# Zero products ahead of the second weight panel: one sequence of three for eight FFNs and three mixers, in place of a table per FFN

## The reference

```python
def swiglu(h, w_gate_up, w_down):
    gate, up = jnp.split(h @ w_gate_up, 2, axis=-1)
    return (jax.nn.silu(gate) * up) @ w_down
```

## Time and profile before

| | |
|---|---|
| median of 3 runs | 2603.05 us (2591.95 to 2603.62) |
| profiled execution, its own time | 2603.65 us |
| its span, first to last instruction | 2601.8 us |
| TensorE busy | 2495.0 us, 96% of the span, 23182 matmuls |
| VectorE busy | 1778.3 us, 68% |
| ScalarE busy | 1259.3 us, 48% |
| mean granted TensorE clock | 0.982 |

### The profile page before, as it was taken

How to read it: one execution, slowest core, us unless ns; L and a number is a source line. 1 busy time by engine, 2 the same in 40 slices (tenths; PEclk the granted TensorE clock), 3 DMA queues, 4 the chain that set the end, 5 groups by cost and what they waited for, 6 DMA issues and landing times.

```text
span 2601.8 us, 54597 instructions
## 1 busy us (share of the span) xinstructions
PE 2495.0 (96%) x23182; PEld 2436.6 (94%) x23182; DVE 1778.3 (68%) x2300; ACT 1259.3 (48%) x1508; POOL 216.0 (8%) x246
## 2 busy tenths in 40 slices
PE   7999759999999899999999999999999999999998
PEld 7999759999999889989999999999999998999998
DVE  5988966556555666657666669876657667986665
ACT  5434445334566653344344346565335335665433
POOL 5000050003000100000000000500000000320000
PEclk9999879999999999999999999999999999999999
DMA  5553014555677735535545544434555554443553
GB/s 214 183 189 125 19 67 176 180 191 169 187 174 182 174 117 193 192 133 189 192 172 206 193 171 154 147 130 165 191 183 185 191 193 147 152 147 146 179 194 127
DMA packets 65839, 430.76 MB, mean 166 GB/s; under 512 B 8288, under 2 KB 11360, under 8 KB 15904
## 3 DMA queue, kind: packets, MB, share of 16 engines
q1 hardware_dynamic: 58864, 410.30, 44.1%
q0 software_dynamic: 6000, 17.46, 4.5%
q10 hardware_dynamic: 832, 0.92, 0.1%
HBM read 426.45 MB, written 1.15 MB: 164 GB/s over the span
## 4 chain that ended last, share of the span: by engine, by line
PE 88%; DVE 7%; ACT 3%; issue 1%; DMA 0%; DVEq 0%; ACTq 0%
PE psum L2020 26%; PE psum L2022 26%; PE psum L2021 26%; DVE w_lo L1332 1%; ACT w_hi L847 1%; PE psum L2070 1%; PE psum L2235 1%; PE psum L2141 1%; PE psum L2384 1%; DVE h L1351 1%; PE psum L2372 1%; DVE h_lo L1340 1%; PE psum L2362 1%; PE psum L2124 0%; PE psum L2328 0%
## 5 line engine op out<-in xcount | busy, mean ns | idle before, releaser
L2020 PE MATMUL psum<-h_hi,w_hi 128*128 128x256 f32 x4320 | 1215.1, 281 | 16.4 <-DVE h_lo L1376 9.6
L2021 PE MATMUL psum<-h_lo,w_hi 128*128 128x256 f32 x4320 | 1205.0, 279 | 0.0
L2022 PE MATMUL psum<-h_hi,w_lo 128*128 128x256 f32 x4320 | 1204.6, 279 | 0.0
L847 ACT ACTIVATE w_hi<-raw 128x2048 fp32r<-128x2048 f32 x387 | 741.2, 1916 | 857.1 <-PE psum L2022 857.1
L1332 DVE TENSOR_TENSOR w_lo<-raw,w_hi 128x2048 fp32r<-128x2048 f32 x387 | 886.8, 2292 | 386.9 <-ACT w_hi L847 386.5
L2020 PEld LDWEIGHTS psum<-h_hi,w_hi 128*128 128x128 f32 x4320 | 816.1, 189 | 26.0 <-issue 20.8
L2021 PEld LDWEIGHTS psum<-h_lo,w_hi 128*128 128x128 f32 x4320 | 815.8, 189 | 0.6 <-issue 0.5
L2022 PEld LDWEIGHTS psum<-h_hi,w_lo 128*128 128x128 f32 x4320 | 815.5, 189 | 0.0
L2020 PE MATMUL psum<-act_hi,w_hi 128*128 128x256 f32 x1536 | 427.3, 278 | 0.7 <-DVE act_lo L1895 0.7
L2021 PE MATMUL psum<-act_lo,w_hi 128*128 128x256 f32 x1536 | 426.1, 277 | 0.0
L2022 PE MATMUL psum<-act_hi,w_lo 128*128 128x256 f32 x1536 | 426.0, 277 | 0.0
(11 more groups left out here) (342 smaller groups left out, 2386.5 us busy)
## 6 DMA issues: line engine op xcount, KB each, us to landing
raw<-in_panels SPq DMA_DIRECT2D x387, 1024.0 KB, 4.8
arena<-bias_by_distance POOLq DMA_DIRECT2D x32, 384.0 KB, 6.2
x<-in_x SPq DMA_DIRECT2D x1, 1024.0 KB, 5.6
arena<-in_s_cbd POOLq DMA_DIRECT2D x4, 256.0 KB, 3.0
arena<-in_s_b SPq DMA_DIRECT2D x1, 1024.0 KB, 15.2
arena<-in_s_c SPq DMA_DIRECT2D x1, 1024.0 KB, 17.2
hidden<-in_s_cbd POOLq DMA_DIRECT2D x4, 256.0 KB, 2.8
arena<-arena POOLq DMA_DIRECT2D x32, 32.0 KB, 1.9
```

Source lines behind the costliest of these rows:

```text
L847: a.activation(w_hi[:, s, :], raw[:, s, :], ACT.Copy).then_inc(hi_ready, 1)
L2020: t.matmul(o, w[0], xin[0], start=start, stop=False, skip_group_check=True)
L2021: t.matmul(o, w[0], xin[1], start=False, stop=False, skip_group_check=True)
L2022: return t.matmul(o, w[1], xin[0], start=False, stop=stop, skip_group_check=True)
```

## The change

The table goes. One sequence, `PACE`, is used in all eight FFNs and in the second panel of both Fourier mixers and of the GLU: the reduced-precision product of 64 columns of zeros ("wide") at (0, 0) and at (0, 4), and the plain fp32 product of two columns ("narrow") at (1, 4). All of them add zeros, so that no result changes.

```diff
-        FFN_LEADS = [{(1, 0): 1}, {(1, 0): 2}, {(0, 4): 0}, {(0, 2): 0, (1, 2): 0}, {(0, 0): 3, (1, 0): 0},
-                     {(0, 0): 2}, {(0, 0): 3, (1, 0): 1}, {(0, 0): 3, (0, 4): 3, (1, 4): 0}]
+        PACE = {(0, 0): True, (0, 4): True, (1, 4): False}
...
-            def lead(o, start=True, form=0):
-                z = zeros[:, :].bitcast(F32)
-                if form == 0:
+            def lead(o, start, wide):
+                if wide:
+                    t.matmul(o[:, 0:E], zeros[:, :], zeros[:, 0:E], start=start, stop=True, skip_group_check=True)
+                else:
+                    z = zeros[:, :].bitcast(F32)
                     t.matmul(o[:, 0:2], z, z[:, 0:2], start=start, stop=True, skip_group_check=True)
-                elif form == 1:
-                    t.matmul(o[:, 0:1], z, z[:, 0:1], start=start, stop=True, skip_group_check=True)
-                elif form == 2:
-                    t.matmul(o[:, 0:S].rearrange("p (a m) -> p a m", a=2), z[0:E, :],
-                             z[0:E, :].unsqueeze(1).to_broadcast([E, 2, P]), start=start, stop=True, skip_group_check=True)
-                else:
-                    t.matmul(o[:, 0:E], zeros[:, :], zeros[:, 0:E], start=start, stop=True, skip_group_check=True)
...
-                project(n0 + 1, 1, led=FFN_LEADS[f])
+                project(n0 + 1, 1, led=PACE)
...
-                    project(st["n0"] + p, p, parts=None if p else (dft_lo_ready, f * KT // 2), frees=(p == 3), led={(0, 0): 0} if p == 1 else None)
+                    project(st["n0"] + p, p, parts=None if p else (dft_lo_ready, f * KT // 2), frees=(p == 3), led=PACE if p == 1 else None)
...
-                    project(st["n0"] + p, p, parts=None if p else (s5_g_lo_ready, 0), frees=(p == 7), led={(0, 0): 0} if p == 1 else None)
+                    project(st["n0"] + p, p, parts=None if p else (s5_g_lo_ready, 0), frees=(p == 7), led=PACE if p == 1 else None)
```

## The result

| | before | changed |
|---|---|---|
| median of 7 runs each | 2603.05 us (2591.95 to 2605.40) | 2578.68 us (2577.45 to 2582.98) |
| profiled execution, own time / span | 2603.65 / 2601.8 us | 2578.26 / 2576.4 us |
| ratio to before, 95% interval | | 0.991 (0.9887 to 0.9933) |

The kernel is 24.4 us faster. The forecast was 2585, the range began at 2580: the direction and the mechanism of the three FFNs were right, the size was not, and the time lies 1.3 us under the range.

The account below looks back on a forecast made before the run. TensorE, busy 96% of the span, was taken as the bound through the spacing of its products. The sum 2603.65 - 20.0 + 0.72 + 0.75 = 2585.1 us was given as 2585, range 2580 to 2599.

Parts of the forecast that it names:

- FFNs 0, 1 and 5 turn quick: From (1, 4) of panel 1, 1500 products per FFN go from 117.8 to 113.3 ns: 6.67 us each, 20.0 saved.
- Turn quick later: FFNs 2, 3, 4, 6 and the three mixers reach the quick pace later, losing 162 products: 0.72 us added.
- the products of zeros themselves: In eight FFNs and three mixers, the zero products cost 4.92 us instead of 4.17: net 0.75 us added.
- I cost this at nothing: In FFN 0, VectorE's low part still arrives before the panel needing it, 0.6 us to spare: no cost.
- Rival 3: FFN 0 falls back to slow after TensorE waits for VectorE at the fifth panel: 2591 us, chance 0.05.
- Rival 1: The narrow product misses in one or two places, each slow FFN costing 6.67 us: 2592 to 2598, chance 0.22.
- rival 2: Something else sets the pace in FFNs 0, 1 and 5, so only costs remain: 2604.4 us, chance 0.08.
- Rival 4: At (1, 4) the narrow product misses where the old table hit, FFNs and mixers turning slow: up to 2634, chance 0.07.
- For this part, which no row prices, I take 4 us to either side.: Stretches between the FFNs at 1.2 GHz can fall differently once everything moves by 7 to 20 us: 4 us either way.

Follow-up runs that it names:

- the early variant: Changed kernel with its sequence replaced by one wide product at (0, 1) and the narrow one at (0, 2), all eleven places: 2630.1 us, 1.0111 of before.

## Why the prediction was right in kind and wrong in size

*"FFNs 0, 1 and 5 turn quick", 6.67 us each:* right. 6.61 measured in each of the three, and in each FFN that changed its pace in any later trace.

*"Turn quick later", 0.72, and "the products of zeros themselves", +0.75:* right, 1.4 measured for the two.

*"I cost this at nothing", VectorE in FFN 0:* right, with 0.5 us to spare where 0.6 were worked out: the low part was there at 90.54 + 2.29 = 92.83, its panel started at 93.32. Rival 3 did not happen. The two lines of the changed kernel:

```profile
90.54 2.29 DVE L1332 TENSOR_TENSOR w_lo<-raw,w_hi 128x2048 fp32r<-128x2048 f32 x1
...
93.32 0.28 PE L2018 MATMUL psum<-h_hi,w_hi 128*128 128x256 f32 x1
```

*Rival 1, a miss in one or two places:* not in the five traces with this sequence, that is in none of 55 places. That was luck in part: the reason given, three hits of three, was a weak one, and the sequence works by the table above, which three rows could not show. The gap in it is a stream that is already quick ahead of the wide product at (0, 4). That happened once, in FFN 0 of the trace with two narrow products, whose sequence is the same up to (1, 4), and there the first narrow one missed: one of 66 places in all.

*Rivals 2 and 4:* rival 2 is out by the first windows view and by the runs with one or two FFNs changed. Rival 4's mechanism exists: the early variant and the narrow product alone are slower than before because the narrow product comes at the wrong place. The changed sequence is not such a case.

*The step that failed* is the base under the sum: "For this part, which no row prices, I take 4 us to either side." It took all stages without a changed product as they were in the one profiled execution, and their shift in time as noise around zero. One of them was no noise. The S5 mixer's start ran at 1.2 GHz for 6.8 us in the kernel before, in both traces, behind a pause of TensorE of 1.48 us. In the three traces of the changed kernel FFN 0 ended some 6 us earlier, the pause was there, and the clock stayed up: 4.3 us in one direction between the profiled pair, 3.1 of them the fall itself. With that term the sum is 2581, inside the range. Why the clock stays up when FFN 0 ends then is open; the runs show only which end times went with which outcome. The other 2.6 us lie in the second Fourier mixer and the second block's mixers of the profiled pair. The second block's two mixers (with their norms) took 495.9 and 493.8 us in the two traces of the kernel before and 493.9, 495.3 and 495.6 in the three of the changed one, so their 2.0 us are the draw of one execution, and no effect of the change is shown in them. The second Fourier mixer's 1.0 us came in all three traces of the changed kernel against both of the kernel before; its cause stays open. A range of 2580 to 2599 was also lopsided: I widened it only for misses, that is upward.

*The table of before was read from one execution.* I took its quick and slow FFNs as properties of their forms. FFN 6 was slow in its second trace, and FFN 5, in its old form, quick in that of the kernel with only FFN 0 changed. Its profiled time of 2603.65, the base of the sum, was a draw among 2590 to 2617, and the changed kernel gains, besides time, a spread of 5.5 us in place of 13.5 (seven runs each).

## What to carry to other kernels

When a long stretch of identical products runs at two paces from one stage to the next, at one granted clock and with no engine waiting, look for what stands at its start, and read more than one execution before a pace is put down to a form. A product that shifts such a stream should be preceded by one that brings it to a known place, and given a settled stream to act on. And when a change moves a stage in time, check the clock in the stages behind it, first of all behind each wait of TensorE: in these traces the same stretch of small products ran at 1.2 or at 2.4 GHz, 3.1 us apart, with the same pause ahead of it.

## What was not expected of the hardware

A stream of alternating weight loads and 256-column products has at least four steady states: one at 113.3 ns a product and three at 117.8 that differ only in which product of three has the longer distance. They last for 1500 products, across panels, and one product of zeros moved the stream between them in a fixed way wherever eleven products stood on each side (the table above). What in TensorE makes them stays open.

The clock fell behind a pause of only 1.48 us, and when TensorE was busy again. Windows of the kernel before, all engines, inside the fall:

```profile
264.60:269.60 5.00, 5.00 (x75) 4.94 (x74) 4.90 (x9) 0.93 (x2) 0.00 (x0) 0.50 0.00 0
```

5.00 of 5.00 us busy at a clock of 0.50. Ahead of it came small products of the S5 mixer (32 rows and 32 columns), then the pause that ended at 263.17, and 0.4 us later, at 263.6, the fall. The Trainium skill, "TensorE: Matmul & The Clock Gate", "Part 1: The HAM clock gate", says that activity releases the throttle. A fall behind a pause agrees with that; why the same pause was followed by a fall in seven traces and not in nine, it does not tell.
